# Sums of a pair's weights moved from GpSimd to VectorE, and the first split weights of a run of pairs moved 64 bytes

## The reference, cut to what matters

```
def swiglu(x, w_gu, w_down):
    gate, up = jnp.split(x @ w_gu, 2, axis=-1)
    return (jax.nn.silu(gate) * up) @ w_down
```

## Time and profile before

| | us |
|---|---|
| median of 3 runs | 3339.61 |
| lowest and highest | 3334.99, 3339.66 |
| the profiled execution | 3338.69 |
| its span, first to last instruction | 3336.9 |
| PE busy | 3292.8 (99%) |
| DVE busy | 2409.7 (72%) |
| ACT busy | 1688.5 (51%) |
| POOL busy | 788.6 (24%) |

### The profile page before, as it was taken

One profiled execution on the slowest core, in us unless ns is written; L12 is line 12 of the kernel. 1 busy time (PEld: TensorE's weight loads), 2 busy tenths in 40 slices (PEclk: granted clock), 3 DMA queues, 4 the chain that ended last, 5 costly groups with the idle time before them and its releaser, 6 DMA issues. The chain is left out here.

```text
span 3336.9 us, 51736 instructions
## 1 busy us (share of the span) xinstructions
PE 3292.8 (99%) x20422; PEld 2934.4 (88%) x20422; DVE 2409.7 (72%) x3946; ACT 1688.5 (51%) x3071; POOL 788.6 (24%) x589
## 2 busy tenths in 40 slices
PE   9999999999999999999999999999999999999998
PEld 7999888888889998999888888899998888888998
DVE  7878765766697778777765766697868676649776
ACT  5445453645455445444553644554547374335443
POOL 2433110121044413432110121043500001204431
PEclk9999999999999999999999999999999999999999
DMA  4323433253223332333423263233332222323332
GB/s 140 108 96 115 116 98 86 80 150 91 86 92 99 110 102 85 102 106 114 120 76 117 59 148 101 67 102 103 111 98 92 87 80 70 109 91 95 98 109 83
DMA packets 118561, 332.79 MB, mean 100 GB/s; under 512 B 18984, under 2 KB 21800, under 8 KB 118320
## 3 DMA queue, kind: packets, MB, share of 16 engines
q1 hardware_dynamic: 106352, 308.40, 29.3%
q0 software_dynamic: 11680, 20.56, 3.1%
q10 hardware_dynamic: 288, 0.52, 0.0%
HBM read 306.23 MB, written 4.21 MB: 93 GB/s over the span
## 5 line engine op out<-in xcount | busy, mean ns | idle before, releaser
L1926 DVE TENSOR_TENSOR wl<-raw,wh 128x1024 fp32r<-128x1024 f32 (+2 forms) x633 | 772.4, 1224 | 274.3 <-ACT wh L1343 268.8
L1343 ACT ACTIVATE wh<-raw 128x1024 fp32r<-128x1024 f32 (+2 forms) x637 | 553.1, 875 | 350.7 <-PE PS L820 324.7
L820 PE MATMUL PS<-bh,wh 128*128 128x256 f32 x2520 | 708.2, 281 | 16.8 <-DVE wl L1926 13.3
L820 PE MATMUL PS<-bh,wl 128*128 128x256 f32 x2520 | 703.6, 279 | 0.0
L820 PE MATMUL PS<-bl,wh 128*128 128x256 f32 x2520 | 703.5, 279 | 0.0
L820 PE MATMUL PS<-uh,wh 128*128 128x512 f32 (+2 forms) x1656 | 613.9, 371 | 10.4 <-DVE ul L1963 3.5
L820 PE MATMUL PS<-ul,wh 128*128 128x512 f32 (+2 forms) x1656 | 599.4, 362 | 0.0
L820 PE MATMUL PS<-uh,wl 128*128 128x512 f32 (+2 forms) x1656 | 599.2, 362 | 0.0
L820 PEld LDWEIGHTS PS<-bh,wh 128*128 128x128 f32 x2520 | 473.2, 188 | 24.9 <-DVE wl L1926 18.2
L820 PEld LDWEIGHTS PS<-bl,wh 128*128 128x128 f32 x2520 | 479.4, 190 | 0.0
L820 PEld LDWEIGHTS PS<-bh,wl 128*128 128x128 f32 x2520 | 473.3, 188 | 0.6
(11 more groups left out here) (268 smaller groups left out, 5693.0 us busy)
## 6 DMA issues: line engine op xcount, KB each, us to landing
raw<-in_gu SPq DMA_DIRECT2D x218, 512.0 KB, 3.2
raw<-in_win SPq DMA_DIRECT2D x139, 512.0 KB, 3.3
raw<-in_dn SPq DMA_DIRECT2D x80, 320.0 KB, 3.0
raw<-in_dn SPq DMA_DIRECT2D x40, 512.0 KB, 3.7
raw<-in_wbr SPq DMA_DIRECT2D x72, 256.0 KB, 2.6
raw<-in_wout SPq DMA_DIRECT2D x24, 512.0 KB, 3.2
raw<-in_dn SPq DMA_DIRECT2D x40, 256.0 KB, 2.7
raw<-in_wv SPq DMA_DIRECT2D x20, 512.0 KB, 3.4
```

Of the source, the lines that this page charges most:

```text
L820: return e.matmul(out, lhs, rhs, start=start, stop=stop, skip_group_check=True)
L1343: return e.activation(out, in_, f, scale=scale, **more)
L1926: tt(lo, src, hi, SUB).then_inc(*S.lo.up(("lo", c)))
```

## The change

A pair that opens a run (f = 4, 10, 15) is called an opening pair; there are 15. POOL goes on making their sums. For the other 75 pairs DVE makes the four sums, in `sum_of_weights`, one of them after each step of the pair before. What waited for POOL's signal for those pairs (ACT's high parts, SP's loads) now waits for DVE's. The `first` cuts of the 15 opening pairs join `HALVED`, so that their high and low parts lie 64 bytes further in the slot.

```diff
--- before.py
+++ after.py
@@ -533,6 +533,7 @@
 
         HALVED = {j.first for v in range(1, 7) for j in sorted((j for j in JOBS.values() if j.tag[1] == v), key=lambda j: j.at)[:3]}
         HALVED |= {j.first for j in JOBS.values() if j.chunks == H2}
+        HALVED |= {j.first for j in JOBS.values() if j.kind == "pair" and (j.tag[2] == PLAIN or j.tag[2] - 1 in PART_AT)}
 
         def split_of(c, a, z):
 
@@ -662,7 +663,7 @@
             kind, p = CUTS[c]
             if kind in ("sums12", "sums43"):
                 s = 1024 if kind == "sums43" else 0
-                return ws[:, s:s + 1024], (S.pl, kind, p)
+                return ws[:, s:s + 1024], summed(kind, p)
             if kind == "last":
                 return raw[:, (p + 1) % 4, 512:1024], (S.raw[(p + 1) % 4], "raw", p + 1)
             return raw[:, p % 4, 0:width(p)], (S.raw[p % 4], "raw", p)
@@ -672,7 +673,13 @@
             c = CUT_OF[p]
             if CUTS[c][0] == "piece":
                 return [(S.lo, "lo", c)]
-            return [(S.lo, "lo", c), (S.pl, "sums43", CUTS[c][1])]
+            return [(S.lo, "lo", c), summed("sums43", CUTS[c][1])]
+
+        OPENING = {CUTS[j.first][1] for j in JOBS.values() if j.kind == "pair" and (j.tag[2] == PLAIN or j.tag[2] - 1 in PART_AT)}
+
+        def summed(kind, p):
+
+            return (S.pl if p in OPENING else S.dn), kind, p
 
         CUT_OF = {}
         for c, (kind, p) in enumerate(CUTS):
@@ -2158,6 +2165,25 @@
                     E.wait_ge(S.dv, "c22", v, f)
                     tt(x, x, tmp[:, f % 2, X0:TW], MUL).then_inc(*S.dv.up(("gated", v, f)))
 
+                def sum_of_weights(f, i):
+
+                    p = CUTS[JOBS["pair", v, f].first][1]
+                    x, y = raw[:, p % 4, :], raw[:, (p + 1) % 4, :]
+                    if i in (1, 3):
+                        E.wait_ge(S.lo, "lo", JOBS["pair", v, f - 1].first + (i + 1) // 2)
+                    if i == 1:
+                        E.wait_ge(S.raw[(p + 1) % 4], "raw", p + 1)
+                        tt(ws[:, 0:512], y[:, 0:512], y[:, 512:1024], ADD).then_inc(*S.dn.up(("sum1", p)))
+                    elif i == 2:
+                        E.wait_ge(S.raw[p % 4], "raw", p)
+                        E.wait_ge(S.dn, "sum1", p)
+                        tt(ws[:, 512:1024], ws[:, 0:512], x[:, 0:512], SUB).then_inc(*S.dn.up(("sums12", p)))
+                    elif i == 3:
+                        tt(ws[:, 1536:2048], x[:, 0:512], y[:, 0:512], SUB).then_inc(*S.dn.up(("sum3", p)))
+                    else:
+                        E.wait_ge(S.dn, "sums12", p)
+                        tt(ws[:, 1024:1536], x[:, 512:1024], ws[:, 512:1024], SUB).then_inc(*S.dn.up(("sums43", p)))
+
                 def part(m, c):
                     job = JOBS["part", v, m, c]
                     ahead(reach(job))
@@ -2208,13 +2234,22 @@
                     ahead(c + 2)
                     if not skip:
                         low_g(f - 1)
+                    follows = f + 1 < FT and f not in PART_AT
+                    if follows:
+                        sum_of_weights(f + 1, 1)
                     ahead(c + 3)
                     if f == PLAIN:
                         low_operand(6)
+                    if follows:
+                        sum_of_weights(f + 1, 2)
                     first_gate(f)
                     ahead(c + 4)
+                    if follows:
+                        sum_of_weights(f + 1, 3)
                     second_gate(f)
                     ahead(c + 5)
+                    if follows:
+                        sum_of_weights(f + 1, 4)
                     next(side, None)
                     if v == 7 and f >= FT - 4:
                         both(2 * (f - FT + 4))
@@ -2838,6 +2873,7 @@
                     a, b = raw[:, p % 4, :], raw[:, (p + 1) % 4, :]
                     if f > PLAIN:
                         E.wait_ge(S.lo, "lo", JOBS["pair", v, f - 1].first + (1 if which == 12 else 2))
+                        E.wait_ge(S.dn, "sums43", CUTS[JOBS["pair", v, f - 1].first][1])
                     if which == 12:
                         E.wait_ge(S.raw[p % 4], "raw", p)
                         E.wait_ge(S.raw[(p + 1) % 4], "raw", p + 1)
@@ -2853,9 +2889,7 @@
                 times_norm(1)
                 times_norm(2)
                 times_norm(3)
-                sums(PLAIN, 12)
-                sums(PLAIN, 43)
-                for f in range(PLAIN + 1, FT):
+                for f in (PLAIN, *(f + 1 for f in PART_AT if f > PLAIN)):
                     sums(f, 12)
                     sums(f, 43)
 
```

## The result

The changed kernel takes 3293.32 us (median of 4 runs, 3291.12 to 3296.73), the kernel before 3338.52 in the 4 runs beside it: a ratio of 0.9866, with a 95% interval from 0.9854 to 0.9877. That is 45.2 us less; 3296 was forecast. The profiled execution took 3291.91 us, with a span of 3290.1 us.

What follows compares the result with a forecast made beforehand. PE was taken as the bound, with DVE binding in stalled pairs. Pairs: 856.8 + 2.2 + 2 + 1.6 = 862.6 us in place of 905.96, 43.4 less, so about 3296 us; range 3289 to 3329.

Steps and rivals of the forecast that it cites:

- DVE's new pair: DVE's time for a pair once it makes the four sums itself: 9.06 us, up to 9.3 with waits.
- 10.24 - 3.58 + 4 x 0.60: DVE's old pair, less the excess length of its instructions beside POOL's, plus four sums made on DVE: 9.06 us.
- The stalls go: In the runs of pairs PE stops waiting for DVE's low part of `last`, a wait of 0.69 us.
- What is late next is nothing: In the pairs no other cut or load comes late for PE: 0.3 us in hand at fast pace, 0.7 at slow.
- The pace: In the runs of pairs the 64-byte shift puts PE at 9.52 us a pair, not 9.89; about 3296 us, chance 0.48.
- the second case: Rival for the runs of pairs: stalls go, 64 bytes change nothing, pairs stay at 9.89 us; 3326 us, chance 0.28.
- each change is a shift of the kind that moved the pace: Distance changes starting products 0 to 3 of each run act like the 0.02 us delay after which PE sped up.
- The price of the shift: Products 0 and 2 of 15 pairs read weights at 128 past, 360 slower matmuls: 0 to 2.4 us, taken as 1.6.
- 360 x 0.007 = 2.4: Upper bound in us for 360 matmuls at 128 past, from 0.130 against 0.123 us each in `v` = 6.
- 3 x 0.74 = 2.2 us: In `v` = 7 three pairs with sums and two more additions take DVE 10.26 us, over PE's fast pace.
- I take 2: In `v` = 0 some six pairs carry up to four small DVE instructions: 0 to 2 us in all, taken as 2.
- The rule on PE: PE never waits on other engines and only DVE and POOL contend, so the shift would do nothing.

Runs made afterwards that it cites:

- POOL's useless additions: The changed kernel with POOL also making four unused additions of 128x512 in each of the 75 pairs: 3495.86 us, ratio 1.0472.

## Why the prediction was right

- **DVE's new pair.** Reckoned at 9.06 us, it is 9.08. The bookkeeping of 10.24 - 3.58 + 4 x 0.60 held because the contended durations were counted as excess over the same shape beside them and not as DVE's own work. The 0.60 for a sum came from the only place where POOL was idle, and it was measured at 0.60. POOL as the cause of the excess, an inference from two durations of one shape, is shown by POOL's useless additions.
- **The stalls go.** Right in all 15 runs. "What is late next is nothing" was right as well, with 0.44 us a pair in hand (9.52 less 9.08), where 0.3 was said. The closest that a low part comes is 0.34 us, in the last run.
- **The pace.** The step with the least behind it, 0.48 against 0.28, came out as forecast: all 15 runs at 9.52. The run without the shift is the second case measured, 3320 where 3326 was given. The reason that I gave for the fast pace, though, was only half right. I argued by the earlier trace rows that "each change is a shift of the kind that moved the pace", as if any disturbance would do. A matmul more does not do it, nor does a change from 0 to 64 past, and short waits do it only at times. What counted was from which distance the stream comes. The fast pace after 128 past is seen in all 15 openings of each of the seven kernels that have such a border there; had the shift been one of 192 bytes, the same argument would have forecast 3293 and met 3323. So the pace was forecast rightly from a reason that does not hold as it stands, and that 64 bytes was the shift to make was luck.
- **The price of the shift.** 15 opening pairs at 9.64 in place of 9.52 are 1.8 us, forecast 1.6. (Its upper bound, "360 x 0.007 = 2.4", multiplies out to 2.5; nothing hangs on it.)
- **The two terms mis-sized.** 862.6 us was forecast for the runs of pairs, 858.6 measured. The 4 us are the terms "3 x 0.74 = 2.2 us" for `v` = 7 and "I take 2" for `v` = 0. Both were 0. In `v` = 7 DVE does take the longer pair as I reckoned it; its timeline, at the two additions of `both`:

```profile
3204.51 1.29 DVE L2051 TENSOR_TENSOR h<-h,y_u 128x512 f32<-128x512 f32 x2
...
3214.79 1.28 DVE L2051 TENSOR_TENSOR h<-h,y_u 128x512 f32<-128x512 f32 x2
```

  They are 10.28 us apart. Yet the last run of the changed kernel lasts 66.75 us, 9.64 + 6 x 9.52 = 66.76. DVE fell 3 x 0.76 = 2.3 us behind and PE never waited, since the low parts are made that much before PE reads them: in this run the one of `sums43` is ready 2.62 us ahead in the second to fourth pair and 0.34 in the last. The mistake was to compare periods where a stretch of only three pairs can be paid out of the lead. It was close. The kernel with two more sums shows the lead used up: after three pairs of 0.88 us each in a run of five, after one in a run of six.
- **The rule on PE.** That only DVE and GpSimd contend (the Trainium skill, SBUF — State Buffer, Who interferes with whom) would have left the shift without effect and the time at the second case. The trace differs: the place of 360 matmuls' weights, 2% of the 20422, moves the whole kernel by 27 us with the same instructions.

**What stays open.** Why PE has two steady paces at 64 past, and what in the stream at 128 past puts it on the fast one. The runs show which changes of place do it, that one added matmul does not, and that short waits do or don't; they show no mechanism. A shift smaller than 64 bytes was not tried, nor other lengths of the stretch at 128 past than 12 matmuls.

## What to carry to other kernels

When one shape of a VectorE instruction with two inputs in SBUF has two durations in a trace, and GpSimd is at work beside the long ones, count the difference as GpSimd's price. Work taken "off" VectorE cost it 3.58 us a pair where making it there costs 2.40. Read PE's pace from start times and not from busy time; where long stretches without any wait differ by some per cent at the same clock, move the operands by 64 bytes, one stretch at a time, and measure: with all the pairs' cuts moved this kernel took 3328 us, with only the openings' 3293. An edit that frees one engine should be measured with the edit that lets the next one use it, since the two here gave 18 and 4 us alone and 45 together.

## What the runs showed of the hardware that I had not expected

- PE's stream of 256-column fp32 matmuls, each with a load of weights of its own, has two steady paces for one and the same code, addresses and clock: 0.1133 and 0.1177 us (9.52 and 9.89 for 84). Without a stall it kept the one it had for up to 588 matmuls.
- Its pace depends on where weights and data lie modulo 256 bytes: 0.1187 at 128 past (9.97 / 84) and 0.120 at 0 past. A border from 128 to 64 past freed the fast pace at once (in all 15 runs of two kernels made to show it), one from 192 to 64 at the second border, one from 0 to 64 not.
- Short waits leave PE on either pace. Of nine of 0.02 to 0.03 us at the fast pace five left it fast and four slow; of nine of 0.03 us at the slow pace four left it fast. Longer stalls have left it on either too.
- POOL's addition of 128x512 adds up to 1.1 us to a VectorE instruction with two inputs in SBUF that runs beside it, nearly twice the 0.60 us that the same addition takes on VectorE.
